# The inverse of the softmax denominators taken over four columns and spread by a copy, and its turn on TensorE moved behind the next scores

## The reference

```python
s = jnp.where(valid[None, :, None, None], s + bias, NEG)                       # windowed
p = jax.nn.softmax(jnp.concatenate([s, sink_logit], axis=-1), axis=-1)[..., :-1]
o = jnp.einsum('bngrqk,bnkgd->bnqgrd', p.astype(v.dtype), vb)

s = (jnp.einsum('bqhd,bkhd->bhqk', qn, k_nope)                                  # latent
     + jnp.einsum('bqhr,bkr->bhqk', qr, k_rot)).astype(jnp.float32) * scale
p = jax.nn.softmax(s, axis=-1)

s = s + Fq[..., None] - F[:, :, None, :]                                        # forgetting
p = jax.nn.softmax(jnp.where(causal, s, -jnp.inf), axis=-1)
o = jnp.einsum('bhqs,bshd->bqhd', p.astype(v.dtype), v)
```

## Time and profile before

| what | value |
|---|---|
| median of 3 runs | 1501.07 us (1500.91 to 1504.25) |
| the profiled execution's own time | 1504.31 us |
| its span | 1502.3 us |
| mean granted clock of TensorE (1.0 is 2.4 GHz) | 0.875 |
| TensorE matmul busy | 1261.3 us (84%) |
| VectorE busy | 695.3 us (46%) |
| ScalarE busy | 461.9 us (31%) |
| GpSimd busy | 271.3 us (18%) |
| chain that ended last | PE 56%, DMA 26%, DVE 9%, POOL 3%, ACT 3% |

### The profile page before, as it was taken

The page is one execution under the profiler, slowest core; times in us unless marked ns, Lnnn a source line. Parts: engine busy times, 40 slices in busy tenths (PEclk is TensorE's granted clock), DMA queues, the critical chain, the costliest instruction groups (busy, mean ns, idle before and its releaser), DMA issues.

```text
span 1502.3 us, 21971 instructions
## 1 busy us (share of the span) xinstructions
PE 1261.3 (84%) x8802; PEld 897.6 (60%) x8802; DVE 695.3 (46%) x1149; ACT 461.9 (31%) x665; POOL 271.3 (18%) x290
## 2 busy tenths in 40 slices
PE   7957897888868887886976768999969978899997
PEld 4535654343324333333844757999959756799996
DVE  2666445221212121123355646766763265477676
ACT  4333322111111011012423315434343332444342
POOL 0000045732032130331314410000016420000000
PEclk9986687787988788888898988999989967899998
DMA  6761187999999999999485123545344300354451
GB/s 255 285 280 56 50 343 329 430 427 430 428 427 429 428 430 428 428 429 403 179 332 219 57 84 113 210 172 200 144 168 168 128 13 15 126 196 181 184 193 42
DMA packets 36000, 369.61 MB, mean 246 GB/s; under 512 B 4070, under 2 KB 5615, under 8 KB 12271
## 3 DMA queue, kind: packets, MB, share of 16 engines
q1 hardware_dynamic: 33552, 364.66, 59.8%
q10 hardware_dynamic: 2398, 4.27, 0.8%
HBM read 367.84 MB, written 1.06 MB: 246 GB/s over the span
## 4 chain that ended last, share of the span: by engine, by line
PE 56%; DMA 26%; DVE 9%; POOL 3%; issue 3%; ACT 3%; DVEq 0%; SPq 0%; ACTq 0%; POOLq 0%
PE ps L642 54%; DMA ring<-in_w_up 23%; DVE W L2088 2%; DMA ring<-in_ada_w 2%; PE ps L657 1%; ACT ring_parts L487 1%; DVE XH L2047 1%; DMA ring<-in_w_in 1%; DVE W L2361 1%; PE ps L887 1%; DMA ring<-in_s_out 1%; DMA ring<-in_fox_in 1%; DVE ring_parts L2119 0%; POOL ring_parts L495 0%; DVE ss L1861 0%
## 5 line engine op out<-in xcount | busy, mean ns | idle before, releaser
L642 PE MATMUL ps<-W_parts 128*128 128x256 f32 (+1 forms) x2672 | 391.0, 309 | 8.0 <-issue 4.3
L642 PEld LDWEIGHTS ps<-W_parts 128*128 128x128 f32 x2672 | 363.3, 194 | 34.6 <-issue 10.2
L642 PE MATMUL ps<-ring,W 128*32 128x512 f32 x1536 | 225.9, 737 | 74.4 <-DMA ring<-in_w_up 44.0
L642 PE MATMUL ps<-W 128*32 128x64 f32 (+6 forms) x1696 | 159.4, 325 | 37.2 <-DVE W L2369 24.5
L642 PEld LDWEIGHTS ps<-ring,W 128*32 128x32 f32 x1536 | 52.4, 128 | 226.5 <-issue 156.1
L495 POOL TENSOR_TENSOR ring_parts<-ring,ring_parts 128x2048 fp32r<-128x2048 f32 x18 | 98.7, 5497 | 362.9 <-ACT ring_parts L487 327.0
L642 PEld LDWEIGHTS ps<-W 128*32 128x32 f32 (+4 forms) x1696 | 103.1, 173 | 95.8 <-issue 83.5
L2395 DVE TENSOR_TENSOR W_parts<-ring,W_parts 128x2048 fp32r<-128x2048 f32 x44 | 100.9, 2293 | 29.8 <-ACT W_parts L1591 29.8
L642 PE MATMUL ps<-XH_parts,ring_parts 128*128 128x256 f32 x512 | 94.3, 287 | 8.5 <-issue 5.0
L2276 DVE COPY W<-ps 128x1024 f32<-128x1024 f32 x16 | 19.6, 1225 | 171.1 <-PE ps L642 171.1
L642 PE MATMUL ps<-ring_parts,W_parts 128*128 128x512 f32 (+1 forms) x288 | 87.2, 411 | 10.5 <-DVE W_parts L2384 10.5
(11 more groups left out here) (363 smaller groups left out, 1447.1 us busy)
## 6 DMA issues: line engine op xcount, KB each, us to landing
ring<-in_w_gate SPq DMA_DIRECT2D x32, 2048.0 KB, 21.8
ring<-in_w_up SPq DMA_DIRECT2D x32, 2048.0 KB, 26.5
ring<-in_w_down SPq DMA_DIRECT2D x32, 2048.0 KB, 23.0
ring<-in_ada_w SPq DMA_DIRECT2D x24, 2048.0 KB, 11.2
ring<-in_up SPq DMA_DIRECT2D x44, 1024.0 KB, 5.6
ring<-in_dn SPq DMA_DIRECT2D x44, 512.0 KB, 3.5
ring<-in_fox_in SPq DMA_DIRECT2D x6, 2048.0 KB, 7.7
ring<-in_w_in SPq DMA_DIRECT2D x2, 2048.0 KB, 13.6
```

Source lines behind the costliest of these rows:

```text
L642: return pe.matmul(o, l, r, start=a, stop=z_, skip_group_check=True, **kw)
```

## The change

Two things change. VectorE first takes the reciprocal of the four columns of `den` in place, waits for it, and then spreads the four results over the 256 columns of `rin` by a copy; the wait for `r_turned`, which guards `rin`, stands between the two. TensorE issues `scores(s + 2)` ahead of `spread(s)` instead of behind it.

```diff
                     turn_probs(2 * s)
                     turn_probs(2 * s + 1)
+                    if s < first + 6:
+
+                        scores(s + 2)
                     spread(s)
-                    if s < first + 6:
-
-                        scores(s + 2)
                     between(s)
                     pe.wait_ge(S("r_copied"), s + 1)
                     outputs(2 * s)
...
+                own(v.reciprocal(den[:, u, a], den[:, u, a]))
                 if s >= 2:
 
                     v.wait_ge(S("r_turned"), s - 1)
-                v.reciprocal(rin[:, s % 2, :].rearrange("p (h d) -> p h d", h=4), bcast(den[:, u, a], [P, 4, 64])
-                             ).then_inc(S("rin_ready"), 1)
+                v.tensor_copy(rin[:, s % 2, :].rearrange("p (h d) -> p h d", h=4), bcast(den[:, u, a], [P, 4, 64])
+                              ).then_inc(S("rin_ready"), 1)
```

More of the change, by code:

```diff
@@ L918, in attention @@
                     turn_probs(2 * s + 1)
-                    spread(s)
                     if s < first + 6:
                         scores(s + 2)
+                    spread(s)
                     between(s)
```

## The result

The changed kernel takes 1460.7 us (median of 4 runs, 1456.76 to 1462.38) where the kernel before takes 1502.66 (4 runs, 1500.91 to 1510.44): a ratio of 0.9707, with a 95% interval of 0.9666 to 0.9749. Timed again on another chip it took 1464.33 (5 runs) beside 1502.53 (9 runs), ratio 0.9748 (0.9727 to 0.9768). It is faster by about 40 us. The forecast was 1473 us with a range of 1463 to 1488.

What follows compares the result with a forecast made beforehand. The attention stages were taken as bound by a back-and-forth chain, TensorE waiting 28.1 us for VectorE's inverses. Less 4.7 and 1.0 that leaves 22.4; plus 6 for the clock, 28 us off 1501.07: 1473 us, range 1463 to 1488.

Steps and rivals of the forecast that it cites:

- The instructions: In VectorE's 16 attention steps, a 4-column reciprocal and a 256-column copy take 0.48 us in place of 1.75.
- slower: Rival for the 16 attention steps: the copy takes as long as the old reciprocal, 1509 us; chance 0.02.
- The order: In both attention stages, scores ahead of the spread fill TensorE's waits; 4.7 us of copy waits open, 1.0 stays in step 6.
- 3.1 to 5.3 us: TensorE's time for transposes and scores before the spread in steps 1 to 4, against about 3.2 us for VectorE's inverses.
- The clock: In both attention stages, with the waits gone, more of TensorE's work falls into full clock; 6 us gained.
- 1.5 tenths: Share of TensorE's 89.9 us of attention work taken to move from 1.2 to 2.4 GHz, at 3.8 us a tenth.
- 4 tenths: Upper end for attention work moving to full clock, 15 us, from where VectorE's loop would bind.
- VectorE's loop of 6 us a step: VectorE's own work in a step of the first attention, said to bind once 4 tenths moved to full clock.
- The clock rises to nearly full: Rival for both attention stages: the clock gives 15 us instead of 6, 37 in all, 1464 us; chance 0.15.
- The clock stays at 1.2 GHz: Rival: the lower clock holds nearly throughout both attention stages; gain 12.2 us, 1489 us; chance 0.17.
- the gain of the first attention is swallowed: Rival behind the first attention: a transfer of independent time hides its gain, only the second's 10 us count, 1491; chance 0.04.

Runs made afterwards that it cites:

- the version with GpSimd: The changed kernel with the four 128x2048 subtractions of steps 0 to 3 moved from VectorE to GpSimd; 1465.76 us, ratio 0.9777 to the kernel before.
- the fills: The kernel before with three unused products, twelve or four unused transposes ahead of each wait for the inverses; 1495.9, 1497.78 and 1496.06 us.

## Why the prediction was too small

**The instructions: right.** The reciprocal takes 171 ns (0.18 said), the copy 293 (0.28). One element read 64 times costs a copy nothing extra; that agrees with the rule of the Trainium skill that the prediction named (Vector Engine (DVE) Microarchitecture Reference, section on performance modes). The rival "slower" needed a copy of about 1.7 us and fell with this row.

**The order: right in kind, somewhat too high in size.** Ten new waits for ScalarE's copy were forecast at 4.7 us; there are ten, for 5.1 (6.9 less the 1.8 that were there). Of the waits for the inverses 1.0 us was to stay, and 4.9 stayed: 1.57 in step 6, where 1.0 was forecast, 2.7 in steps 1, 3 and 4 and 0.6 in step 14, where none was forecast. The fault here is the step that let TensorE need "3.1 to 5.3 us" to the spread: it took the durations of a TensorE at the clock as it was. At full clock transposes and scores take 2.2 to 2.8 (from 106.23 and from 124.55 on), and in steps 1 to 4 VectorE's 3.2 us end later. So standing gave 18.6 us and not 22.4.

**The clock: the step that failed.** The prediction said "I take 1.5 tenths, 6 us, nearer to none, since at 151.58 and 154.39 TensorE was busy for long and still ran at the lower level". Measured are 24.6 us, by its own price of 3.8 us a tenth 6.4 tenths of the work; in the inner stretches alone 24.4 (76.18 us of busy time before, 51.75 after) and, in the second execution of the changed kernel, 21.2 (54.94). Its upper end, 4 tenths, was too low as well. That end came from VectorE's loop of 6 us a step, which is real but is found only in steps 1 to 4 of the first stage; it was applied to all sixteen. The reason given for taking so little doesn't hold either. The dense work at 151.58 and 154.39 was read as a sign that full clock stays away from such work. With twelve transposes in each wait and nothing else changed, the scores and outputs of that step ran at full clock (2.92 us in place of 5.30) and its transposes partly (1.60 in place of 1.97). So such work can have it. Why it did not in the kernel before is open: the level stayed low there through 13.4 us of work, so the prediction's sentence that it "rises behind one of work" is too simple as well.

**The rivals.** "The clock rises to nearly full" was what happened, at 0.15, and its 1464 was the nearest of all the numbers: inside the range of the second timing, above that of the first. In part that is luck: it had 15 us for the clock, 10 too few, and 22.4 for the standing, 4 too many. "The clock stays at 1.2 GHz" fell. So did "the gain of the first attention is swallowed": the routing's last copy starts 30.8 us earlier and the experts' last copy out of PSUM 30.5 earlier (656.7 in place of 687.2).

**The sum.** Forecast: 22.4 + 6 = 28 us. Measured in the profiled executions: 18.6 + 24.6, and 1.8 around them, 45.0. By the medians it is 42.0 and 38.2.

## What to carry to other kernels

In a stage where an engine chain goes back and forth, the waits of TensorE have to be priced twice: by their length, and by what the stage's work would save if it went from its time at the granted clock to its time at 2.4 GHz. Here the second was the larger, 24.6 us against 18.6. Where the profile shows such a stage at a clock near 0.67, take as upper end all of its work at full clock, and check only where another engine would bind, step by step. Unused work put into the waits is a cheap experiment that shows before anything is rewritten whether the clock has a share, though here it gave back only 11 us of it.

## What the runs showed of the hardware that was not expected

**VectorE is held by GpSimd, even for 4 columns.** In the version with GpSimd, the four VectorE instructions with two inputs in SBUF that met one of GpSimd's subtractions ended within 0.02 us of its end, and took up to 4.42 us instead of 0.16. Beside the same subtractions neither the maxima nor the normalization, which read PSUM, was longer:

```profile
104.17 0.42 DVE L2057 CUSTOM_DVE_ANT_0 XH<-ps,W 128x256 f32<-128x256 f32 x1 [1.13 <-PE ps L642]
...
116.64 0.42 DVE L2108 TENSOR_TENSOR W<-ps,W 128x256 f32<-128x256 f32 x1 [0.65 <-PE ps L642]
```

This agrees with the Trainium skill (SBUF — State Buffer, "two separate sides"): the port pair that both share is locked for the whole instruction, also against a VectorE instruction with two SBUF inputs.

**One kernel, two clocks.** The second stage of the changed kernel ran 24.83 us at 0.96 in one execution and 28.59 at 0.79 in another, with the same waits (0.6 us for L2089; 3.9 and 3.8 for L1343). In the first, TensorE's work went to 2.4 GHz at about 1196.5, in step 9; in the other at about 1207.5, in step 11. What sets this is open. It is also a measure of what can't be read from one profile: some 4 us.

**Work behind the experts varies with no edit in it.** From the experts' last copy out of PSUM to the second stage it is 528.4 us before, 530.8 and 532.4 in the two executions of the changed kernel, and 536.1 with twelve transposes. TensorE's busy time for the same products between the routing's last copy and the second stage is 811.4, 816.2, 820.5 and 817.2 us in these four, so again a part of it is clock. Which execution gets which is open, and so is why the fills arrived only by half.
